# The last stage of a hybrid retention, state-space and expert layer: another split of the tokens over partitions, grouped transfers and a shared product

## The reference, cut to what matters

```python
x = x + g1 * rmsnorm(y, norm_post_mix[l])            # after the mixer: "x1" in the kernel
h = rmsnorm(x, norm_pre_ffn[l]) * (1.0 + sc2) + sh2
out = hier_moe(h.reshape(b * L, d), ...)             # two experts for each token, summed
x = x + g2 * rmsnorm(out.reshape(b, L, d), norm_post_ffn[l])
```

## Time and profile before

| | us |
|---|---|
| median of 3 runs | 2351.19 (2348.69 to 2351.74) |
| the profiled execution, its own time | 2347.74 |
| its span | 2346.1 |
| experts stage's last TensorE work ends | about 2287.2 |
| combine: first load issued | 2299.42 |
| combine: last VectorE instruction ends | about 2342.9 |

### The profile page before, as it was taken

How to read it: one execution, slowest core, us unless ns; L and a number is a source line. 1 busy time by engine, 2 the same in 40 slices (tenths; PEclk the granted TensorE clock), 3 DMA queues, 4 the chain that set the end, 5 groups by cost and what they waited for, 6 DMA issues and landing times. The chain is left out here.

```text
span 2346.1 us, 35420 instructions
## 1 busy us (share of the span) xinstructions
PE 2171.1 (93%) x11594; PEld 1835.1 (78%) x11595; DVE 1413.0 (60%) x2099; ACT 1055.8 (45%) x1518; POOL 652.2 (28%) x647
## 2 busy tenths in 40 slices
PE   8999999999999679997999959999999999999890
PEld 5888888899998568886888847778788888887770
DVE  6322222377554568886577764865766765647776
ACT  4422332243223036664332224765666665547763
POOL 0000000000000658886222222322333333323323
PEclk9999999999999989998999969999999999999995
DMA  8632333546551986665553336997988888868998
GB/s 307 233 110 109 126 145 136 187 156 213 180 172 59 349 329 231 224 223 190 168 215 139 118 95 181 346 291 238 348 277 258 272 267 257 243 177 273 350 349 307
DMA packets 297516, 518.78 MB, mean 221 GB/s; under 512 B 33406, under 2 KB 206022, under 8 KB 292664
## 3 DMA queue, kind: packets, MB, share of 16 engines
q1 hardware_dynamic: 271000, 439.52, 54.8%
q0 software_dynamic: 17216, 44.60, 8.5%
q10 hardware_dynamic: 9216, 33.56, 3.5%
HBM read 397.28 MB, written 129.09 MB: 224 GB/s over the span
## 5 line engine op out<-in xcount | busy, mean ns | idle before, releaser
L2528 DVE TENSOR_TENSOR e_w_low<-e_w_whole,e_w_high 128x2048 fp32r<-128x2048 f32 x192 | 431.1, 2287 | 92.8 <-ACT e_w_high L2480 92.1
L2480 ACT ACTIVATE e_w_high<-e_w_whole 128x2048 fp32r<-128x2048 f32 x192 | 357.6, 1914 | 44.3 <-DMA e_w_whole<-in_moe_w_down_dram 20.0
L2419 PE MATMUL e_pG<-e_w_high,e_xT 128*128 128x512 f32 x768 | 299.9, 390 | 1.2 <-ACT e_xT L2473 1.2
L2420 PE MATMUL e_pG<-e_w_low,e_xT 128*128 128x512 f32 x768 | 299.7, 390 | 0.0
L859 PE MATMUL proj_acc<-w_high,hT_high 128*128 128x512 f32 x672 | 264.4, 394 | 0.0
L859 PE MATMUL proj_acc<-w_low,hT_high 128*128 128x512 f32 x672 | 262.4, 391 | 0.0
L859 PE MATMUL proj_acc<-w_high,hT_low 128*128 128x512 f32 x672 | 262.3, 390 | 0.0
L2428 PE MATMUL e_pY<-e_w_high,e_hT 128*128 128x512 f32 x768 | 225.4, 405 | 18.4 <-ACT e_hT L2492 18.4
L2423 PE MATMUL e_pG<-e_w_high,e_xT 128*128 128x512 f32 x768 | 189.9, 389 | 0.0
L2428 PEld LDWEIGHTS e_pY<-e_w_high,e_hT 128*128 128x128 f32 x768 | 137.8, 189 | 46.0 <-ACT e_hT L2492 20.8
L2419 PEld LDWEIGHTS e_pG<-e_w_high,e_xT 128*128 128x128 f32 x768 | 144.8, 189 | 31.8 <-issue 1.6
(11 more groups left out here) (302 smaller groups left out, 4194.0 us busy)
## 6 DMA issues: line engine op xcount, KB each, us to landing
e_w_whole<-in_moe_w_gate_dram SPq DMA_DIRECT2D x64, 1024.0 KB, 8.5
e_w_whole<-in_moe_w_up_dram SPq DMA_DIRECT2D x64, 1024.0 KB, 11.2
e_w_whole<-in_moe_w_down_dram SPq DMA_DIRECT2D x64, 1024.0 KB
by_token<-tok SPq DMA_DIRECT2D x32, 512.0 KB, 3.0
w_in_raw<-in_w_mod_dram SPq DMA_DIRECT2D x32, 512.0 KB, 4.4
m_tok<-by_token SPq DMA_DIRECT2D x16, 768.0 KB, 5.5
s_kv<-by_token SPq DMA_DIRECT2D x20, 512.0 KB, 6.1
modulated_high<-hT_high SPq DMA_DIRECT2D x9, 1024.0 KB, 3.9
```

The costliest lines, as they stand in the source:

```text
L2419: nc.tensor.matmul(pG[:, half], xT[:, 0, k], wh[:, half, w], start=(k == 0), stop=False)
L2420: nc.tensor.matmul(pG[:, half], xT[:, 0, k], wl[:, half, w], start=False, stop=False)
L2480: nc.scalar.activation(wh[:, third, part], raw[:, third, part], ACT.Copy).then_inc(whs.sem, 1)
L2528: nc.vector.tensor_tensor(wl[:, third, part], raw[:, third, part], wh[:, third, part].bitcast(F32), ALU.subtract).then_inc(wls.sem, 1)
```

## The change

- `LOADS` and `STORES` replace 16 loads by six (of 1, 1, 2, 4, 4, 4 tiles) and 16 stores by seven (2, 2, 4, 4, 2, 1, 1 tiles). `by_rows` gives partition p the tokens 16p to 16p+15, and tile t is token t of each: a partition's rows lie side by side in device memory, so a transfer of four tiles has pieces of 16 KB. x1 is read in the same way: three transfers of 2 MB for the twelve tiles, one for the other four.
- `c_yy` lies where the experts' split weights are, and SP issues the loads at the end of the experts stage's program, when GpSimd has seen the last scatter land (`summed_up`). SP no longer waits for x1 there; VectorE does, before its first line-2625 instruction.
- The gain product of tiles 2, 5, 8, 11 and 14 is done by GpSimd, behind the root of its pair of tiles. VectorE waits for it before it uses that tile.

```diff
@@ experts
+        g["c_yy_at"] = nc.sbuf_base
...
-        x1_early = kit.landing("c_x1_early_in", dmas=NL)
+        g["x1_early"] = x1_early = kit.landing("c_x1_early_in", dmas=4)
+        g["c_y_in"] = kit.landing("c_y_in", len(LOADS))
+        summed_up = kit.counter("c_rows_summed")
+        g["c_yy"] = kit.at("c_yy", [P, NL, D], g["c_yy_at"])
...
-            for t in range(EARLY, NL):
-                sp.dma_start(early_x1(g, t), dram["x1"][t]).then_inc(x1_early.sem(0), 16)
+            sp.dma_start(g["x1_rest"][:], by_rows(dram["x1"].rearrange("t p d -> (t p) d"), EARLY, NL)).then_inc(x1_early.sem(0), 16)
...
                 sp.wait_ge(wls.sem, wls.at(NE - 1, 2 * third + 2))
-                for t in range(4 * third, 4 * third + 4):
-                    sp.dma_start(early_x1(g, t), dram["x1"][t]).then_inc(x1_early.sem(0), 16)
-            sp.wait_ge(x1_early.sem(0), x1_early.at(0))
+                to = raw[:, third].rearrange("p (t d) -> p t d", t=4)
+                sp.dma_start(to, by_rows(dram["x1"].rearrange("t p d -> (t p) d"), 4 * third, 4 * third + 4)).then_inc(x1_early.sem(0), 16)
+
+            sp.wait_ge(summed_up.sem, summed_up.at(0))
+            for n, (t, last) in enumerate(LOADS):
+                sp.dma_start(g["c_yy"][:, t:last], by_rows(dram["ys"][0:SEQ], t, last)).then_inc(g["c_y_in"].sem(n), 16)
...
                 scatter(b + n)
                 landed(b + n)
+            pool.sem_inc(summed_up.sem, 1)
@@ combine
+LOADS = ((0, 1), (1, 2), (2, 4), (4, 8), (8, 12), (12, 16))
+STORES = ((0, 2), (2, 4), (4, 8), (8, 12), (12, 14), (14, 15), (15, 16))
+
+def by_rows(rows, t, last):
+    return rows.rearrange("(p t) d -> p t d", t=NL)[:, t:last]
...
+        def by_pool(t):
+            return t % 3 == 2
+        def gain(t):
+            return (yy[:, t], yy[:, t], g["mod"][:, 3], ALU.mult)
...
-            for t in range(NL):
-                sp.dma_start(yy[:, t], dram["ys"][t * P:(t + 1) * P, :]).then_inc(y_in.sem(t), 16)
-            for t in range(NL):
-                sp.wait_ge(outs.sem, outs.at(t))
-                sp.dma_start(io["out0"][0, t * P:(t + 1) * P, :], yy[:, t]).then_inc(o_out.sem(0), 16)
+            to = by_rows(io["out0"].rearrange("o n d -> (o n) d"), 0, NL)
+            for t, last in STORES:
+                sp.wait_ge(outs.sem, outs.at(last - 1))
+                sp.dma_start(to[:, t:last], yy[:, t:last]).then_inc(o_out.sem(0), 16)
...
                 rstd_root(nc, g, pool, eps_added, n, 1, ss[:, 1, span], ss[:, 0, span], D).then_inc(rstd.sem, 1)
+                for t in range(n * GROUP, (n + 1) * GROUP):
+                    if by_pool(t):
+                        nc.gpsimd.tensor_tensor(*gain(t)).then_inc(gained_pool.sem, 1)
...
-            def gain(t):
-                dve.wait_ge(ssq.sem, ssq.at(t))
-                nc.vector.tensor_tensor(yy[:, t], yy[:, t], g["mod"][:, 3], ALU.mult).then_inc(gained.sem, 1)
+            def own_gain(t):
+                if not by_pool(t):
+                    dve.wait_ge(ssq.sem, ssq.at(t))
+                    nc.vector.tensor_tensor(*gain(t)).then_inc(gained.sem, 1)
...
+            dve.wait_ge(x1_early.sem(0), x1_early.at(0))
             for t in range(NL):
                 if t + GROUP < NL:
-                    gain(t + GROUP)
+                    own_gain(t + GROUP)
                 dve.wait_ge(rstd.sem, rstd.at(t // GROUP))
-                dve.wait_ge(gained.sem, gained.at(t))
+                if by_pool(t):
+                    dve.wait_ge(gained_pool.sem, gained_pool.at(nth(t)))
+                else:
+                    dve.wait_ge(gained.sem, gained.at(nth(t)))
```

More of the change, by code:

```diff
@@ L2575, in combine @@
     with ExitStack() as st:
-        yy = kit.sb("c_yy", [P, NL, D], stack=st)
+        kit.fill("c_fill_first", 2048, st)
+        assert nc.sbuf_base == g["c_yy_at"]
+        kit.sb("c_yy_room", [P, NL, D], stack=st)
+        yy = g["c_yy"]
         sq = kit.sb("c_sq", [P, D], stack=st)
         ss = kit.sb("c_ss", [P, 2, NL], stack=st)
-        y_in = kit.landing("c_y_in", NL)
-        o_out = kit.landing("c_out", dmas=NL)
+        y_in = g["c_y_in"]
+        x1_early = g["x1_early"]
+        o_out = kit.landing("c_out", dmas=len(STORES))
         ssq = kit.counter("c_ssq")
@@ L2584, in combine, with nth @@
         gained = kit.counter("c_rows_gained")
+        gained_pool = kit.counter("c_rows_gained_by_pool")
         outs = kit.counter("c_out_ready")
         block = st.enter_context(nc.Block())
+        def by_pool(t):
+            return t % 3 == 2
+        def nth(t):
+            return sum(by_pool(n) == by_pool(t) for n in range(t))
+        def gain(t):
+            return (yy[:, t], yy[:, t], g["mod"][:, 3], ALU.mult)
         @block.sync
         def _(sp):
-            for t in range(NL):
-                sp.dma_start(yy[:, t], dram["ys"][t * P:(t + 1) * P, :]).then_inc(y_in.sem(t), 16)
-            for t in range(NL):
-                sp.wait_ge(outs.sem, outs.at(t))
-                sp.dma_start(io["out0"][0, t * P:(t + 1) * P, :], yy[:, t]).then_inc(o_out.sem(0), 16)
+            to = by_rows(io["out0"].rearrange("o n d -> (o n) d"), 0, NL)
+            for t, last in STORES:
+                sp.wait_ge(outs.sem, outs.at(last - 1))
+                sp.dma_start(to[:, t:last], yy[:, t:last]).then_inc(o_out.sem(0), 16)
             sp.wait_ge(o_out.sem(0), o_out.at(0))
@@ L2598, in _ @@
         def _(act):
[L2599 to L2603, removed]
+            for n, (t0, last) in enumerate(LOADS):
+                act.wait_ge(y_in.sem(n), y_in.at(0))
+                for t in range(t0, last):
+                    if t:
+                        act.wait_ge(ssq.sem, ssq.at(t - 1))
+                    nc.scalar.activation(sq[:], yy[:, t], ACT.Square, accum_out=ss[:, 0, t:t + 1]).then_inc(ssq.sem, 1)
         @block.gpsimd
@@ L2610, in _ @@
                 rstd_root(nc, g, pool, eps_added, n, 1, ss[:, 1, span], ss[:, 0, span], D).then_inc(rstd.sem, 1)
+                for t in range(n * GROUP, (n + 1) * GROUP):
+                    if by_pool(t):
+                        nc.gpsimd.tensor_tensor(*gain(t)).then_inc(gained_pool.sem, 1)
         @block.vector
         def _(dve):
-            def gain(t):
-                dve.wait_ge(ssq.sem, ssq.at(t))
-                nc.vector.tensor_tensor(yy[:, t], yy[:, t], g["mod"][:, 3], ALU.mult).then_inc(gained.sem, 1)
+            def own_gain(t):
+                if not by_pool(t):
+                    dve.wait_ge(ssq.sem, ssq.at(t))
+                    nc.vector.tensor_tensor(*gain(t)).then_inc(gained.sem, 1)
             for t in range(GROUP):
-                gain(t)
+                own_gain(t)
+            dve.wait_ge(x1_early.sem(0), x1_early.at(0))
             for t in range(NL):
                 if t + GROUP < NL:
-                    gain(t + GROUP)
+                    own_gain(t + GROUP)
                 dve.wait_ge(rstd.sem, rstd.at(t // GROUP))
-                dve.wait_ge(gained.sem, gained.at(t))
+                if by_pool(t):
+                    dve.wait_ge(gained_pool.sem, gained_pool.at(nth(t)))
+                else:
+                    dve.wait_ge(gained.sem, gained.at(nth(t)))
                 nc.vector.scalar_tensor_tensor(out=yy[:, t], in0=yy[:, t], scalar=ss[:, 1, t:t + 1], in1=early_x1(g, t), op0=ALU.mult, op1=ALU.add).then_inc(outs.sem, 1)
```

## The result

| | before | after |
|---|---|---|
| median of 12 runs each | 2348.97 (2345.08 to 2351.74) | 2352.43 (2347.96 to 2356.72) |
| the profiled execution | 2347.74 | 2356.72 |
| its span | 2346.1 | 2355.1 |

The changed kernel takes 1.0016 times as long, 95% interval 1.0009 to 1.0024: +3.5 us on the medians, on the slow side; the interval just reaches past 0.2%. Forecast were 2355.1, 2348 to 2359, "within 0.2%". The forecast time is 2.7 us above the measured one, and 2.2 of that is the base: the three runs of before that I had lay that much above the median of twelve.

The account below looks back on a forecast made before the run. VectorE's chain was taken to bound the last stage, after a hole behind the last scatter. Terms -4.1 + 0.9 + 3.1 + 2.8 + 1.2 gave +3.9 us on 2351.19, so 2355.1 us, range 2348 to 2359.

Parts of the forecast that it names:

- part 5: Experts' end: x1's 16 KB pieces delay the scatter beside them by 3.7 us, 2.4 of it slack; +1.2 us taken.
- Part 1: Start of last stage: loads issued at the last scatter's landing, before the engines' meeting, bring VectorE's first gain forward; -4.1 us.
- Part 2: Last stage's loads: a tile waits for its whole group, so VectorE loses +0.9 us, bounds 0 and +2.4.
- Part 3: Last stage: five GpSimd products hold VectorE off, 1.76 us each for 1.14 saved; +3.1 us, bounds -5.7 and +4.3.
- Part 4: Kernel's end: the store of tiles 8 to 11 leaves late, so the tail behind VectorE grows from 3.2 to 6.0; +2.8 us.
- the 1 us of waiting for GpSimd: Last stage, sign of being wrong: VectorE idles for GpSimd by more than 1 us in all.
- Side by side: Rival, last stage: GpSimd's products don't hold VectorE; 2347.5 us, or 2346.3 without part 5; chance 10%.
- GpSimd becomes the bound: Rival, last stage: GpSimd's chain of roots and products sets the end; +8.2 us, 2359.4; chance 20%.
- Slower transfers: Rival, last stage's DMA: rows 64 KB apart slow transfers; at 300 GB/s +6.9 us, 2358; chance 6%.
- The change doesn't do what it says: Rival, start of last stage: longer meeting or SP's issues keep the first square at 2303.6 or later; +8.0, 2359.2; 7%.

Follow-up runs that it names:

- e1: Changed kernel, but VectorE makes all sixteen gain products and GpSimd none: 2344.84 us, before on the same chip 2344.23.
- e9: e3, but the six loads are issued after the engines have met, without SP's wait for `summed_up`: 2347.45 us, before on the same chip 2348.46.
- e10: e3, but sixteen early loads of one tile instead of six: 2348.36 us, before on the same chip 2348.83.
- e3: Changed kernel, but VectorE makes all gain products and there are sixteen single stores: 2344.09 us against 2348.46 before, ratio 0.9981.
- e6: e5, but GpSimd's five extra instructions are memsets of the same tile instead of products: 2344.38 us, before on the same chip 2348.83.
- e8: e3, but twelve tiles of x1 come in twelve transfers with 4 KB pieces: 2349.10 us, before on the same chip 2348.46.
- e7: Changed kernel, but gain row and VectorE's gained tiles in PSUM, gains waiting only for loads, seven loads, sixteen stores: 2342.18 us against 2348.46 before, ratio 0.9972.
- e2: Changed kernel, but with sixteen stores of one tile; GpSimd's products stay: 2347.90 us, before on the same chip 2344.23.
- e5: Changed kernel, but VectorE makes all gains and GpSimd makes five extra products nobody waits for: 2356.70 us, before on the same chip 2344.23.
- e4: Changed kernel, but VectorE's eleven gains read the gain row from a PSUM copy; GpSimd's five products stay: 2350.66 us, before on the same chip 2344.23.

## Why the prediction was right

By the sum: +3.9 us forecast on the span, +4.0 measured from the scatter's issue, +3.5 on the medians. That the sum comes so near is luck. The products cost 1.8 us more than forecast, and part 5, forecast at +1.2, did not show at all; with two smaller terms that were 0.4 too large and one 0.3 off the other way, they cancel. Measured from the mark, which leaves part 5 out, the forecast was +2.7 and the result +4.05. There the terms are -3.8 (first gain), +0.5 (late groups, e1 against before), +4.9 (products, after against e1) and +2.4 (tail, after against before): 4.0.

- **Part 1, loads early, -4.1: right.** The first gain moved from 17.51 to 13.70 us behind the mark, -3.8, in which 0.3 are lost again by a last scatter of 6.3 instead of 6.1 us; e9 gives -4.5 for the whole. The six issues ended in time (2.85 us; I had 3.4), and e10 shows what happens when they don't. That the meeting stays was right.
- **Part 2, late groups, +0.9: the mechanism right, the size within what repeats.** ScalarE did run dry (3.03 us). Where VectorE makes all gains, its stretch is longer than before by 0.3 (e3), 0.5 (e1, e6) or 0.9 us (e8, e9), though e10, with no groups, has 0.3 as well; beside the products nothing that can be seen: its wait of 0.96 us at 2313.93 lies wholly under GpSimd's product of 2312.30 to 2315.18, during which VectorE couldn't have worked. The landings came a little sooner than laid out, mostly because the first did: 3.5 us after its issue in place of 4.2, and 12.5 for tiles 4 to 7 in place of 12.9.
- **Part 3, products, +3.1: the mechanism right, the price too low.** The step was "a product on GpSimd then takes 1.76 us out of VectorE's time". It takes 2.1 to 2.2; the net is +4.9 to +5.1, outside the bound of 4.3 that I gave. The 1.76 came from a product of the mixing stage, whose like takes 1.90 us; the one of this stage takes 2.35 where nothing holds it (e7). I priced one product by another because both are 128x1024, but in the source of the mixing stage both operands are broadcasts of smaller tiles (line 1534), and here both are whole tiles or rows. That this makes the difference is not shown. About 1.0 of the 4.9 us is idle time more than in e1, which I had not counted: 0.96 for the first root, just under the 1 us of waiting for GpSimd that I had named as a sign of being wrong. The Trainium skill, "GPSIMD Engine Reference", section 3.1, puts such a product at 1.96 times VectorE's time, which I had set aside for the row; 2.35 against VectorE's 1.217 is 1.93, so the page was nearer. (I had set the 1.76 us beside the ratio 1.96; as a ratio the row's is 1.76 to 1.217, or 1.45.)
- **Part 4, grouped stores, +2.8: right.** +2.4 in the tail against before, +2.6 between after and e2. The store of tiles 8 to 11 went out 5.9 us before VectorE's end, as worked out, and the DMA was full from its first bytes on (0.92 and 1.01 of the stretches from 2344, of which the first begins 0.4 us ahead of the bytes). Its 8 tiles took 10.0 us from first to last byte, at the 420 GB/s that I had taken; the 0.3 us that are missing lie behind the last byte (0.7 to the end of the span, where I had 1.0). What I didn't see is that the term hangs on part 3: without the products it is 1.4.
- **Part 5, x1 in 16 KB pieces, +1.2: too large.** The scatter was delayed by 2.5 to 3.2 us against before in the ten kernels with 16 KB pieces of x1 (by 3.3 in e3 against e8), where I had 3.7; the slack was 2.9, where I had 2.4. In the changed kernel nothing shows, with 0.1 us left; in e1, where the scatter was slowest, 0.3 us do. Had the delay been as I worked it out, 0.8 us would have.

The rivals. *Side by side* is out as the kernel stands (e5), and true where the operands are in PSUM (e7). *GpSimd becomes the bound* was half right: the chain of waits now runs through GpSimd (the product and the root's two lines, 2644, 214 and 216, follow one another without a gap), though each took what I had counted, 2.85 and 1.14 + 1.61. But e5 shows that products that nobody waits for cost nearly the same, 2.03 us, so the bound is the time that one engine holds the other off, not GpSimd's place in the chain. GpSimd's small instructions are held off too, so its three tiles take the same 8.0 us as VectorE's (2317.97 to 2325.98). *Slower transfers* is out: 432 GB/s by the landings. *The change doesn't do what it says* is out for the meeting, which didn't grow.

What stays open: the rate's part in the result (no kernel had grouped loads with 4 KB pieces), what each of e7's edits gives, and whether the meeting's 4.15 us (below) can be had; taking it away wasn't tried.

## What to carry to other kernels

Before giving a share of one elementwise loop to GpSimd, look at whether both engines read SBUF with two operands at once; if they do, the share can cost VectorE more than it saves (here 2.0 to 2.2 us for a gain of 1.14). Moving one operand to PSUM in one of VectorE's two instructions was not enough (e4); with both moved, but for five tiles, and the other edits of e7, the share paid. Price an instruction by a row of the same operands, not only of the same shape. Group transfers where the number of issues stands in front of something (e10), and keep them single where each can leave when its producer is done (e3 against e1).

## What the runs showed of the hardware that I had not expected

- The hole between the last scatter's landing and the release of the engines, which I couldn't name, is one GpSimd instruction. The views leave out some instructions, but the trace has them: GpSimd's last one in the experts stage, a DRAIN, begins 0.2 to 0.3 us after the last scatter has landed and takes 4.151 us in all twelve kernels, with loads in flight or not. In before and after, the engines are released 0.2 to 0.3 us behind it. Another on line 1793, near 1380 us, takes 2.997 in before, after, e1, e3, e9 and e10. What the two wait for is not shown.
- By the landings, four tiles in 16 KB pieces take 4.84 to 4.85 us, 432 to 433 GB/s (after, e1, e3); a tile in 4 KB pieces takes 1.28 us before and 1.26 on average in e10 (tiles 5 to 13), 411 and 416. The Trainium skill, "DMA: Bandwidth & Descriptors", section "Where 436 GB/s comes from", gives about 358 for transfers between device memory and SBUF; all of these are above that, so the measurement decides.
- The same large pieces on SP's queue hold up a scatter of GpSimd's: 12.5 to 13.2 us to land in ten kernels instead of 10.0 (before) and 9.4 (e8).
- GpSimd's 128x2 addition of the first root takes 1.22 us beside a VectorE gain that reads two operands from SBUF (before, after) and 0.19 beside one that has its row in PSUM (e4, e7); the power behind an addition takes up to 1.61 in before and after and often 0.69 to 0.70 in e4 and e7. In e1 two such powers take 2.75. The small instructions are held off as the large ones are.
